# Output-gate projection moved between the samples' score products, last score product and sigmoid moved behind the stage's barrier, prompt stores moved between weight loads

## The chip, the cores and the metric

The kernel runs on one core of a Trainium2 chip. The metric is the time of one execution on the device in microseconds (us); lower is better. The profile names the engines PE (TensorE matmul), PEld (its weight load), DVE (VectorE), ACT (ScalarE), POOL (GpSimd) and SP (SyncE). All data is float32. Each float32 matmul of the program appears in the trace as two records.

## The reference

One layer of a network runs over 512 prompt tokens and over 8 decoding sequences ("samples") of 8 tokens each, 576 tokens in all. Every token row `h` is multiplied by one wide matrix `w_in`, and the parts feed an mLSTM branch, a dilated-window attention branch and two merge gates. What the change touches:

```python
parts = jnp.split(h @ prm['w_in'], split_points, axis=-1)
qk, conv_new = _causal_conv(parts[0], conv_s, prm['conv_w'], prm['conv_b'])   # then silu
ipre = (parts[3] + prm['b_igate'])                                            # 4 heads
logf = jax.nn.log_sigmoid(parts[4] + prm['b_fgate'])                          # 4 heads
hm, C1, n1, m1 = _mlstm_chunkwise(qm, km, vm, ipre, logf, C0, n0, m0)
hm = hm * jax.nn.sigmoid(parts[2])                                            # output gate
...
# per sample and head, for three window groups over cached keys and values
s = jnp.einsum('bthd,btjhd->bthj', q, kg) * (q.shape[-1] ** -0.5)
p, lse = _softmax_lse(jnp.where(valid, s, -inf))
```

Prompt attention over three windows (128, 512 and 2048 with dilations 1, 4, 16), the rolled key and value caches of the samples, and a PEER expert layer complete the step. The prompt's keys and values and the rolled caches are outputs.

## The kernel before

The program is a sequence of blocks. In a block each engine has its own list of instructions, ordered by hand, and semaphores tie them together. A block ends with a barrier over all engines. The token rows are held transposed in `k.hT` (8 slices of 128 features by 576 tokens); token tiles are four of 128 and one of 64 (`NCH` = 5).

**prompt_attention** (355 to 552 us of the trace) runs 16 steps `s`, one for each of 4 token tiles and 4 heads. TensorE does in step `s`: the scores of step `s + 1` (L662), `first_pieces[s]` pieces of projection work, the transposes of the probabilities of step `s` (L676), one more piece, and the product with the values (L683). The transposes wait for VectorE's normalised probabilities (`s_norm`), the value product for ScalarE's copy of the transposes (`s_te`, L720). ScalarE does the exponentials of step `s + 1` (L729) before that copy. Tiles 0 to 3 have 3, 6, 8 and 10 key blocks of 128.

A piece is one unit of **MlstmProjections**: 8 accumulating matmuls into bank 6 or 7, and an eviction by ScalarE (`take`, L600 to L608). The weights come in 8 loads of 1 MB through a ring of two slots (`load`, L571): loads 0 to 3 hold the q/k parts (4 pieces each, L584, 288 columns), loads 4 and 5 the values and 6 and 7 the output gate (5 pieces each, L587, 256 columns). The output gate's pieces are evicted with a sigmoid into `m.o`, all others with a copy. With `first_pieces = [2] * 4 + [1] * 12` steps 0 to 3 take three pieces and steps 4 to 15 two. Load `n` is issued when the last piece of load `n - 2` is done.

On SyncE's queue the stores of the prompt's keys and values (`kT_p` L643, `v_p` L644, three pairs, 1 MB each) follow the eighth load. GpSimd's queue issues three copies of 1 MB each from cache to cache in HBM in every step (`rolls`, L653; the last eight are of 480 KB); these are the rolled caches.

**conv_and_gates** (552 to 657 us) computes three things side by side. VectorE and ScalarE run the causal convolutions, the silu, and the chain of the gate rows. TensorE begins with new-key scores and zeros (L842, L832), then the products of the two gates (L1037: 4 output rows, 512 + 64 columns, one gate after the other), with the score products of **SampleAttention** (`product(n)` for sample `n`, L867) after them. One product is 104 matmuls of 128 columns in three parts whose cached keys arrive in a ring of three slots (1.25, 1 and 1 MB), so part `n` is requested when part `n - 3` has been used. It writes to 32-row groups of the output, four heads side by side. After sample 4 come the transposes of the gate rows (L1049, L1052), then samples 5 to 7. VectorE masks the scores (`masked`, L880 to L884), ScalarE takes their exponentials (L889), and the barrier follows. SyncE also loads the first sample's values (`CG_LOADS`), stores the small output `m_new` and waits until it has landed.

**mlstm_and_merge** (from 657 us) begins with `scores(0)` (L1339 to L1341), the transposes of the samples' probabilities (`sa.turn`, L905, L906, after VectorE's `normalised`), and `sums(0)` (L1356 on). Then the samples' value products, the mLSTM chunks and the merge units alternate. The output block and the expert layer follow to the end.

## Time and profile before

| | us |
|---|---|
| median of 3 runs (lowest, highest) | 2494.43 (2490.22, 2497.33) |
| the profiled execution | 2489.25 |
| its span | 2487.5 |
| PE busy | 2159.1 (87%) |
| DVE busy | 1232.5 (50%) |
| ACT busy | 762.6 (31%) |
| POOL busy | 733.8 (29%) |

The busy shares average over stages with different limits. The expert layer takes the last two thirds of the span, so what matters for the change is read from the two blocks that it touches, between 355 and some 670 us. A row of the trace in time gives start, duration, engine, line, operation, what is written from what, and the count of instructions merged; a bracket gives idle time before it and what ended that.

### The profile page before, as it was taken

The page shows a single profiled execution, that of the slowest core. Times are in us where ns is not written, and L with a number is a line of the kernel's source. Part 1 is how long each engine was busy: PE and PEld are TensorE (multiplying, and loading weights), DVE is VectorE, ACT ScalarE, POOL GpSimd, SP SyncE. Part 2 cuts the span into 40 slices and gives each one's busy share as a digit, 9 for nine tenths or more (in the row PEclk, how much of TensorE's full clock was granted, in tenths as well). Part 3 has the DMA queues.
Part 4 walks back from the last instruction along what each step waited for, and adds up shares of the span by engine and source line. Part 5 has one row for each costly group of instructions (what it writes and reads, how often), then busy time and mean ns, then how long its engine had stood idle before and what let it go on. Part 6 is the DMA issues. An engine that isn't in the chain of part 4 may idle for free.

```text
span 2487.5 us, 25285 instructions
## 1 busy us (share of the span) xinstructions
PE 2159.1 (87%) x9074; PEld 1247.8 (50%) x9074; DVE 1232.5 (50%) x3183; ACT 762.6 (31%) x2197; POOL 733.8 (29%) x694
## 2 busy tenths in 40 slices
PE   6999989997799879999997888787879787978686
PEld 3777448875588545555553443343434333433221
DVE  1000001216233156556666766677676766676764
ACT  2000012242132034444334443343333333333322
POOL 0000001110102014334344444343434352444341
PEclk8999999997699989999999989898989898989899
DMA  9566648888786559999999999999999999999997
GB/s 357 208 242 259 255 168 320 321 299 342 267 298 229 200 225 394 390 396 408 390 381 400 420 403 396 419 416 415 419 413 420 413 412 409 398 420 420 420 419 295
DMA packets 125489, 875.53 MB, mean 352 GB/s; under 512 B 15944, under 2 KB 17256, under 8 KB 40500
## 3 DMA queue, kind: packets, MB, share of 16 engines
q0 software_dynamic: 85760, 691.32, 69.0%
q1 hardware_dynamic: 38652, 182.48, 19.4%
q8 instruction: 71, 1.16, 0.2%
q14 instruction: 54, 0.44, 0.0%
q10 hardware_dynamic: 952, 0.13, 0.0%
HBM read 861.53 MB, written 99.37 MB: 386 GB/s over the span
## 4 chain that ended last, share of the span: by engine, by line
PE 34%; DVE 14%; DMA 13%; issue 2%; ACT 2%; POOL 1%; ACTq 0%; POOLq 0%; DVEq 0%
PE ps L1888 24%; DMA pr_ring<-in_uv,pr_idx 12%; PE ps L1784 3%; DVE pr_ring L2110 3%; PE ps L1824 3%; PE ps L1833 1%; PE ps L1846 1%; PE ps L1806 1%; DVE pr_hot L2090 1%; DVE pr_hot L2094 1%; DVE pr_ind L2071 1%; DVE pr_ind L2068 1%; DVE pr_pick L2097 1%; DVE pr_val L2070 1%; ACT pr_coef L1960 1%
## 5 line engine op out<-in xcount | busy, mean ns | idle before, releaser
L1888 PE MATMUL ps<-pr_ring,pr_diag 128*128 128x512 f32 (+1 forms) x2224 | 1042.8, 623 | 210.5 <-ACT pr_diag L1964 210.3
L1769 POOL DMA_INDIRECT pr_ring<-in_uv,pr_idx x556 | 640.0, 1151 | 956.5 <-PE ps L1888 815.6
L2110 DVE CUSTOM_DVE_ANT_0 pr_ring<-pr_ring,h 128x1024 f32<-128x1024 f32 x556 | 662.7, 1223 | 357.7 <-DMA pr_ring<-in_uv,pr_idx 356.6
L1888 PEld LDWEIGHTS ps<-pr_ring,pr_diag 128*128 128x128 f32 (+1 forms) x2224 | 424.3, 195 | 773.9 <-issue 473.0
L1955 ACT ACTIVATE pr_gel<-pr_dots 128x2 f32<-128x2 f32 x288 | 58.0, 201 | 526.0 <-DVE pr_dots L2110 525.2
L1964 ACT ACTIVATE pr_diag<-ident,pr_coef 128x128 f32<-128x128 f32 x512 | 173.6, 386 | 0.0
L1960 ACT ACTIVATE pr_coef<-pr_gel,pr_wgt 128x1 f32<-128x1 f32 x576 | 138.4, 287 | 27.0 <-ACT pr_gel L1955 0.4
L1784 PE MATMUL ps<-trunk,pr_wq 128*128 128x320 f32 (+2 forms) x544 | 131.7, 396 | 3.0 <-ACT trunk L1990 2.2
L474 PE MATMUL ps<-trunk,ap_ring 128*128 128x288 f32 x384 | 126.3, 411 | 2.9 <-PEq L192 2.9
L475 PE MATMUL ps<-trunk,ap_ring 128*128 128x288 f32 x384 | 125.2, 408 | 0.0
L1784 PEld LDWEIGHTS ps<-trunk,pr_wq 128*128 128x128 f32 x544 | 100.0, 194 | 41.6 <-issue 14.9
L435 POOL DMA_DIRECT2D out_win_s<-in_cache x39 | 19.2, 493 | 328.5 <-PE ps L475 238.1
L474 PEld LDWEIGHTS ps<-trunk,ap_ring 128*128 128x128 f32 x384 | 72.9, 191 | 23.8 <-issue 4.2
L867 PE MATMUL ps<-sa_ring,sa_spread 128*32 128x128 f32 x1664 | 64.5, 316 | 23.4 <-DMA sa_ring<-in_kcacheA 14.4
L475 PEld LDWEIGHTS ps<-trunk,ap_ring 128*128 128x128 f32 x384 | 73.5, 192 | 20.5
L478 PE MATMUL ps<-ap_ring,trunk 128*128 128x512 f32 x192 | 83.6, 594 | 0.0
L697 DVE CUSTOM_DVE_ANT_0 pa_prob<-ps,pa_masks 128x256 f32<-128x256 f32 (+3 forms) x48 | 19.4, 455 | 128.6 <-PE ps L662 128.6
L491 DVE COPY vS<-ps 64x512 f32<-64x512 f32 x3 | 2.1, 693 | 151.9 <-PE ps L466 151.9
L653 POOL DMA_DIRECT2D out_win_s<-in_cache x49 | 23.5, 486 | 175.8 <-PE ps L676 175.6
L1955 ACT ACT_TABLE_LOAD x58 | 74.4, 1283 | 1.1
L587 PE MATMUL ps<-mp_ring,trunk 128*128 128x256 f32 (+1 forms) x320 | 72.6, 380 | 0.0
L379 DVE TENSOR_TENSOR late_rows<-ps,late_bias 128x512 f32<-128x512 f32 x2 | 1.4, 692 | 141.6 <-PE ps L369 141.6
(319 smaller groups left out, 2306.5 us busy)
## 6 DMA issues: line engine op xcount, KB each, us to landing
out_win_s<-in_cache POOLq DMA_DIRECT2D x64, 1020.0 KB, 7.7
sa_ring<-in_cache SPq DMA_DIRECT2D x24, 1024.0 KB, 9.1
side_unit<-in_w_merge SPq DMA_DIRECT2D x32, 768.0 KB, 7.1
late_ring<-in_w_ada SPq DMA_DIRECT2D x8, 2048.0 KB, 17.4
sa_ring<-in_kcacheB SPq DMA_DIRECT2D x16, 1024.0 KB, 7.5
pr_wq<-in_peer_wq SPq DMA_DIRECT2D x16, 1024.0 KB, 8.8
out_win_s<-in_cache POOLq DMA_DIRECT2D x16, 1008.0 KB, 9.5
ap_ring<-in_w_attn_qk SPq DMA_DIRECT2D x6, 2048.0 KB, 21.1
```

The source lines that it names most:

```text
L474: pe.matmul(ps[:, u % 2, 0:TH], wc, rhsT[:, c, 0:TH], **on)
L475: mm = pe.matmul(ps[:, 2 + u % 2, 0:TH], wc, rhsT[:, c, TH:T], **on)
L478: mm = pe.matmul(ps[0:r, u % 2, :], rhsT[:, c, tile_cols(j)], w[:, c, :], **on)
L587: mm = pe.matmul(self.k.ps[0:tile_rows(j), bank, 0:self.WIDE], hT[:, c, tile_cols(j)], w[:, c, :], **on)
L1769: pool.indirect_dma_start(row(n), None, d["uv"], bass.IndirectOffsetOnAxis(ap=idx[:, b % 4, j:j + 1], axis=0)).then_inc(arrived[slot(n)], 16)
L1784: mm = pe.matmul(ps[:, QUERY_BANK, 0:cols.stop - cols.start], e.wq[:, c, piece % 2 * P:(piece % 2 + 1) * P], e.h2T[:, c, cols], start=c == ...
L1824: mm = pe.matmul(ps[:, SIDE_BANK, 0:REST], front.unit[:, u % 2, c, :], k.hT[:, c, rest_cols], start=c == 0, stop=c == KD - 1)
L1888: mm = pe.matmul(ps[0:r, bank + half, :], diag[:, slot(n), 0:r], row(n)[:, o:o + CHUNK], start=h == 0 and j == 0, stop=b == FINAL[i] and j ...
L1955: act.activation(gel[:, o:o + BATCH], dots[:, o:o + BATCH], ACT.Gelu).then_inc(s_gel, 1)
L1960: act.activation(coef[:, o + j:o + j + 1], gel[:, o + j:o + j + 1], ACT.Copy, scale=wgt[:, b % 4, at:at + 1]).then_inc(s_cf, 1)
L1964: act.activation(diag[:, o + j, 0:r], k.ident[:] if i < PT else k.fold[:], ACT.Copy, scale=coef[:, o + j:o + j + 1]).then_inc(s_dg, 1)
L2110: ins = dve.tensor_tensor_reduce(u, u, e.h2[:, BLOCKS[b][0], :], 1.0, 0.0, ALU.mult, ALU.add, dots[:, slot(n):slot(n) + 1])
```

## The change

Five things move.

- MlstmProjections makes 6 loads. The ten output-gate pieces leave the prompt attention; `first_pieces` is `[2] * 4 + [1] * 2 + [0] * 10`, so that steps 4 and 5 keep two pieces and steps 6 to 15 have one, behind the transposes.
- The ten pieces become `output_gate(u)` in conv_and_gates: two before the first sample's product, then one after each of samples 0 to 3, one before each of samples 5 and 6, and two at the end. Their weights have one buffer `ow`, loaded twice. ScalarE evicts them with a copy; one sigmoid over all of `m.o` runs at the head of the next block.
- The score product of sample 7, `masked` and the exponentials move behind the barrier. The first sample's values are loaded there too.
- The two gates' products are written in four 32-row groups of bank 0 (two gates by two halves of 288 tokens), interleaved, where they stood one after the other.
- The three pairs of prompt stores are issued behind weight loads 2, 3 and 4; the store of `m_new` no longer ends the block.

```diff
-        self.loads = 8
+        self.loads = 6
...
-    def load(self, sp):
-        for n in range(self.loads):
+    def load(self, sp, loads):
+        for n in loads:
...
-                out, how = (m.v, ACT.Copy) if n < 6 else (m.o, ACT.Sigmoid)
-                ins = act.activation(out[0:r, j, o:o + self.WIDE], res[0:r, 0:self.WIDE], how)
+                ins = act.activation(m.v[0:r, j, o:o + self.WIDE], res[0:r, 0:self.WIDE], ACT.Copy)
...
-        first_pieces = [2] * 4 + [1] * 12
+        first_pieces = [2] * 4 + [1] * 2 + [0] * 10
         with nc.Block() as block:
             @block.sync
             def _(sp):
-                mp.load(sp)
+                mp.load(sp, range(mp.SLOTS))
                 for g in range(G):
+                    mp.load(sp, range(mp.SLOTS + g, mp.SLOTS + g + 1))
                     sp.dma_start(d["kT_p"][g], a.qk[:, (2 * g + 1) * H:(2 * g + 2) * H, :]).then_inc(s_kv, 16)
                     sp.dma_start(d["v_p"][g], a.v[:, :, g, :]).then_inc(s_kv, 16)
+                mp.load(sp, range(mp.SLOTS + G, mp.loads))
                 sp.wait_ge(s_kv, 16 * 2 * G)
...
+GATES = ((1, 0), (1, 1), (0, 0), (0, 1))
-CG_LOADS = (NS + 1) * SampleAttention.PARTS
+CG_LOADS = NS * SampleAttention.PARTS
...
-                for dst, src in ((state[:], "stateT"), (cw[:], "conv_w"), (wg[:], "w_gates"), (gb[:], "b_gates"),
-                                 (m0[:], "m0"), (carry[:], "c_carry"), (restart[:], "c_restart")):
+                sp.dma_start(wg[:], d["w_gates"]).then_inc(s_wg, 16)
+                for dst, src in ((state[:], "stateT"), (cw[:], "conv_w"), (gb[:], "b_gates")):
                     sp.dma_start(dst, d[src]).then_inc(s_in, 16)
+                sp.dma_start(ow[:], d["w_mlstm"][6]).then_inc(ow_ready, 16)
+                for dst, src in ((m0[:], "m0"), (carry[:], "c_carry"), (restart[:], "c_restart")):
+                    sp.dma_start(dst, d[src]).then_inc(s_in, 16)
+                sa.load(sp, range(sa.SR))
                 for dst, src in ((m.tri[:], "c_tri"), (m.stri[:], "c_stri"), (m.mhg[:], "mh_norm_g")):
                     sp.dma_start(dst, d[src]).then_inc(m.s_const, 16)
-                sa.load(sp, range(sa.SR))
-                sp.dma_start(smask[:].rearrange("p q n -> p (q n)"), d["c_smask"]).then_inc(sa.s_mask, 16)
+                sp.dma_start(sa.smask[:].rearrange("p q n -> p (q n)"), d["c_smask"]).then_inc(sa.s_mask, 16)
                 sa.load(sp, range(sa.SR, 4 * sa.PARTS))
+                sp.wait_ge(s_om, NCH)
+                sp.dma_start(ow[:], d["w_mlstm"][7]).then_inc(ow_ready, 16)
                 sp.wait_ge(s_new, 2)
                 sp.dma_start(d["conv_p"], newp[:]).then_inc(s_out, 16)
                 sp.dma_start(d["conv_s"], news[:]).then_inc(s_out, 16)
-                sa.load(sp, range(4 * sa.PARTS, CG_LOADS))
+                sa.load(sp, range(4 * sa.PARTS, 6 * sa.PARTS))
                 sp.wait_ge(s_mn, 2)
-                sp.dma_start(d["m_new"], mnew[:]).then_inc(s_out, 16)
-                sp.wait_ge(s_out, 48)
+                sp.dma_start(d["m_new"], m.new[:]).then_inc(m.s_new, 16)
+                sa.load(sp, range(6 * sa.PARTS, CG_LOADS))
+                sp.wait_ge(s_out, 32)
...
-                pe.wait_ge(s_in, 7 * 16)
-                for gate in (1, 0):
-                    for part, cols in ((0, slice(0, SEQ)), (1, slice(SEQ, T))):
-                        n = cols.stop - cols.start
-                        for c in range(KD):
-                            mm = pe.matmul(ps[0:H, 2 * gate + part, 0:n], wg[:, c, gate * H:(gate + 1) * H],
-                                           k.hT[:, c, cols], start=c == 0, stop=c == KD - 1)
-                    mm.then_inc(s_gm, 1)
-                    sa.product(pe, 1 - gate)
-                for n in range(2, 5):
+                pe.wait_ge(s_wg, 16)
+                def output_gate(u):
+                    j = u % NCH
+                    if j == 0:
+                        pe.wait_ge(ow_ready, 16 * (u // NCH + 1))
+                    if u >= 3:
+                        pe.wait_ge(s_ot, u - 2)
+                    for c in range(KD):
+                        mm = pe.matmul(ps[0:tile_rows(j), 1 + u % 3, 0:WIDE], k.hT[:, c, tile_cols(j)], ow[:, c, :],
+                                       start=c == 0, stop=c == KD - 1)
+                    mm.then_inc(s_om, 1)
+
+                for step in range(KD):
+                    for j, (gate, half) in enumerate(GATES):
+                        mm = pe.matmul(ps[32 * j:32 * j + H, 0, 0:TH], wg[:, step, gate * H:(gate + 1) * H],
+                                       k.hT[:, step, half * TH:(half + 1) * TH], start=step == 0, stop=step == KD - 1)
+                mm.then_inc(s_gm, 1)
+                output_gate(0)
+                output_gate(1)
+                for n in range(4):
                     sa.product(pe, n)
+                    output_gate(n + 2)
+                sa.product(pe, 4)
                 pe.wait_ge(s_exp, 1)
...
-                for n in range(5, NS):
+                for n in range(5, NS - 1):
+                    output_gate(n + 1)
                     sa.product(pe, n)
+                for u in range(NS, 2 * NCH):
+                    output_gate(u)
...
+                def output_gates(us):
+                    for u in us:
+                        j, o = u % NCH, u // NCH * WIDE
+                        r = tile_rows(j)
+                        act.wait_ge(s_om, u + 1)
+                        act.activation(m.o[0:r, j, o:o + WIDE], ps[0:r, 1 + u % 3, 0:WIDE], ACT.Copy).then_inc(s_ot, 1)
+
+                chain.step(gate_rows(1, fg))
...
-                for b in range(H):
-                    silu(b)
+                output_gates(range(0, 2))
+                silu(0)
+                output_gates(range(2, 3))
+                silu(1)
+                output_gates(range(3, 4))
+                silu(2)
+                silu(3)
+                output_gates(range(4, 5))
                 act.wait_ge(s_rows, 1)
                 for kind in (W_, E_, X_):
                     act.activation(m.rows[:, kind, :], m.rows[:, kind, :], ACT.Exp)
                 act.activation(m.decay[:], m.decay[:], ACT.Exp).then_inc(s_exp, 1)
-                for b in range(H, 2 * H):
-                    silu(b)
-                sa.exponentials(act)
+                output_gates(range(5, 6))
+                silu(4)
+                output_gates(range(6, 7))
+                silu(5)
+                output_gates(range(7, 8))
+                silu(6)
+                silu(7)
+                output_gates(range(8, 2 * NCH))
...
-                sa.masked(dve, chain, smask)
...
                 mg.load(sp, 1)
+                cache(NS)
                 cache(NS + 1)
...
+                sa.product(pe, NS - 1)
                 scores(0)
                 sa.turn(pe)
...
+                act.activation(m.o[:, 0:PT, :], m.o[:, 0:PT, :], ACT.Sigmoid)
+                act.activation(m.o[0:TS, PT, :], m.o[0:TS, PT, :], ACT.Sigmoid).then_inc(m.s_o, 1)
+                sa.exponentials(act)
...
+                sa.masked(dve, chain)
                 sa.normalised(dve, chain)
...
+                    if c == 0:
+                        dve.wait_ge(m.s_o, 1)
```

On TensorE, the last full step of the prompt attention (scores L662/L663, transposes L676/L677, projection pieces L587, values L683/L684). Before:

```order
L662 MATMUL ps<-a_qk 128x256
L662 MATMUL ps<-a_qk 128x512 x2
L587 MATMUL ps<-mp_ring,trunk 128x256 x8
L676 MATMUL ps<-ident,pa_prob 128x128 x10
L587 MATMUL ps<-mp_ring,trunk 128x256 x8
L683 MATMUL ps<-pa_probT,a_v 128x128 x10
```

With the change:

```order
L663 MATMUL ps<-a_qk 128x256
L663 MATMUL ps<-a_qk 128x512 x2
L677 MATMUL ps<-ident,pa_prob 128x128 x10
L587 MATMUL ps<-mp_ring,trunk 128x256 x8
L684 MATMUL ps<-pa_probT,a_v 128x128 x10
```

The piece ahead of the transposes is gone.

On TensorE, the whole of conv_and_gates, from the new-key scores to the next block's first product (L1037/L1058 gates, L867/L870 score products, L1052 with `cg_ow` the output-gate pieces). Before:

```order
L842 MATMUL ps<-qkS 32x64 x24
L832 MATMUL ps<-trunk,sa_spread 32x384 x8
L1037 MATMUL ps<-trunk,cg_wg 4x512 x8
L1037 MATMUL ps<-trunk,cg_wg 4x64 x8
L867 MATMUL ps<-sa_ring,sa_spread 32x128 x52
L1037 MATMUL ps<-trunk,cg_wg 4x512 x8
L1037 MATMUL ps<-trunk,cg_wg 4x64 x8
L867 MATMUL ps<-sa_ring,sa_spread 32x128 x208
L1049 MATMUL ps<-ident,m_rows 128x4 x16
L1049 MATMUL ps<-ident,m_rows 64x4 x4
L1052 MATMUL ps<-m_decay,sel 128x12 x4
L867 MATMUL ps<-sa_ring,sa_spread 32x128 x156
```

With the change (two blocks of rows, the second from the transposes of the gate rows on):

```order
L845 MATMUL ps<-qkS 32x64 x24
L835 MATMUL ps<-trunk,sa_spread 32x384 x8
L1058 MATMUL ps<-trunk,cg_wg 4x288 x32
L1052 MATMUL ps<-cg_ow,trunk 128x256 x16
L870 MATMUL ps<-sa_ring,sa_spread 32x128 x52
L1052 MATMUL ps<-cg_ow,trunk 128x256 x8
L870 MATMUL ps<-sa_ring,sa_spread 32x128 x52
L1052 MATMUL ps<-cg_ow,trunk 128x256 x8
```

```order
L1073 MATMUL ps<-ident,m_rows 128x4 x16
L1073 MATMUL ps<-ident,m_rows 64x4 x4
L1076 MATMUL ps<-m_decay,sel 128x12 x4
L1052 MATMUL ps<-cg_ow,trunk 128x256 x8
L870 MATMUL ps<-sa_ring,sa_spread 32x128 x52
L1052 MATMUL ps<-cg_ow,trunk 128x256 x8
L870 MATMUL ps<-sa_ring,sa_spread 32x128 x52
L1052 MATMUL ps<-cg_ow,trunk 128x256 x8
L1052 MATMUL ps<-cg_ow,trunk 64x256 x8
L1006 UNCONDITIONAL_BRANCH
L1381 UNCONDITIONAL_BRANCH
L870 MATMUL ps<-sa_ring,sa_spread 32x128 x52
```

The output-gate pieces stand between the score products, and the last 52 score matmuls behind the two branches that are the barrier.

On SyncE, the prompt attention's weights and stores. Before:

```order
L571 DMA mp_ring<-in_w_mlstm 128x2048 x8
L643 DMA out_kT_p<-a_qk 128x2048
L644 DMA out_v_p<-a_v 512x1x512
L643 DMA out_kT_p<-a_qk 128x2048
L644 DMA out_v_p<-a_v 512x1x512
```

With the change:

```order
L571 DMA mp_ring<-in_w_mlstm 128x2048 x3
L643 DMA out_kT_p<-a_qk 128x2048
L644 DMA out_v_p<-a_v 512x1x512
L571 DMA mp_ring<-in_w_mlstm 128x2048
L643 DMA out_kT_p<-a_qk 128x2048
L644 DMA out_v_p<-a_v 512x1x512
L571 DMA mp_ring<-in_w_mlstm 128x2048
```

The stores stand between loads that TensorE still needs.

## Rows read from the trace of the kernel before

**Rows 1.** Stretches of the program: busy us per engine, clock, DMA share, GB/s.

```profile
355.00:552.00 197.00, 195.38 (x996) 159.43 (x996) 37.84 (x160) 61.15 (x132) 23.54 (x49) 0.98 0.86 312
552.00:657.00 105.00, 69.93 (x1009) 47.82 (x1009) 45.58 (x142) 20.38 (x30) 9.76 (x7) 0.69 0.79 303
...
900.00:2487.00 1587.00, 1339.93 (x3500) 648.64 (x3500) 1050.91 (x2572) 578.08 (x1797) 659.53 (x574) 0.93 0.99 404
```

**Rows 2.** TensorE in time, one prompt-attention step: start, us, line, operation, count.

```profile
530.91 3.62 PE L587 MATMUL ps<-mp_ring,trunk 128*128 128x256 f32 x16
534.36 1.26 PE L676 MATMUL ps<-ident,pa_prob 128*128 128x128 f32 x10
535.45 3.62 PE L587 MATMUL ps<-mp_ring,trunk 128*128 128x256 f32 x16
538.91 2.39 PE L683 MATMUL ps<-pa_probT,a_v 128*128 128x128 f32 x20
```

**Rows 3.** ScalarE in time, in that same step.

```profile
533.18 1.36 ACT L729 ACTIVATE pa_prob<-pa_prob,pa_nb 128x1280 f32<-128x1280 f32 x1 [2.64 <-DVE pa_nb L702]
...
534.65 1.28 ACT L608 ACT_TABLE_LOAD   x1
...
536.23 1.36 ACT L720 ACTIVATE pa_probT<-ps 128x512 f32<-128x512 f32 x3
```

**Rows 4.** TensorE in time, projection pieces at the start of the prompt attention.

```profile
374.66 7.93 PE L584 MATMUL ps<-trunk,mp_ring 128*128 128x288 f32 x32
...
387.97 7.93 PE L584 MATMUL ps<-trunk,mp_ring 128*128 128x288 f32 x32
...
415.84 4.04 PE L584 MATMUL ps<-trunk,mp_ring 128*128 128x288 f32 x16
...
437.94 3.62 PE L587 MATMUL ps<-mp_ring,trunk 128*128 128x256 f32 x16
```

**Rows 5.** Issue to landing by tile: weights, key stores, value stores.

```profile
DMA to landing us min/median/max: 4.7/9.6/15.8
...
DMA to landing us min/median/max: 20.4/34.7/44.0
...
DMA to landing us min/median/max: 29.8/30.5/42.3
```

**Rows 6.** DMA queues, 510 to 540 us: packets, MB, share of 16 engines.

```profile
q0 software_dynamic: 254, 6.10, 53.6%
q1 hardware_dynamic: 1832, 5.16, 44.0%
```

**Rows 7.** TensorE in time, conv_and_gates to the start of mlstm_and_merge.

```profile
555.58 1.50 PE L842 MATMUL ps<-qkS 128*32 128x64 f32 x48 [3.70 <-PEq L2282]
...
561.08 9.53 PE L1037 MATMUL ps<-trunk,cg_wg 128*4 128x512 f32 x31
...
570.49 3.00 PE L867 MATMUL ps<-sa_ring,sa_spread 128*32 128x128 f32 x101
...
603.04 1.08 PE L867 MATMUL ps<-sa_ring,sa_spread 128*32 128x128 f32 x32 [0.91 <-DMA sa_ring<-in_kcacheB]
...
611.74 1.94 PE L867 MATMUL ps<-sa_ring,sa_spread 128*32 128x128 f32 x32 [0.65 <-DMA sa_ring<-in_kcacheB]
...
656.84 0.45 PE L1339 MATMUL ps<-ident,m_qk 128*128 128x128 f32 x1 [8.72 <-PEq L1000]
```

**Rows 8.** Three engines in time, last score product to first sums.

```profile
648.29 0.56 DVE L880 TENSOR_TENSOR sa_sc<-ps,cg_smask 128x384 f32<-128x384 f32 x1 [18.30 <-PE ps L867]
...
652.91 0.19 ACT L889 ACTIVATION_READ_ACCUMULATOR sa_sc<-sa_sc,sa_nb 128x1 f32 x1
...
657.04 1.36 DVE L896 TENSOR_TENSOR sa_sc<-sa_sc,sa_rden 128x1152 f32<-128x1152 f32 x1
...
663.82 0.69 DVE L1471 TENSOR_TENSOR ml_w<-m_tri,ps 128x512 f32<-128x512 f32 x1 [5.42 <-PE ps L1341]
...
666.59 0.57 PE L1356 MATMUL ps<-m_v,ml_sT 128*128 128x128 f32 x2 [0.32 <-DVE ml_sT L1477]
```

More of the change, by code:

```diff
@@ L1061, in _, with gate_rows @@
                 act.wait_ge(s_gm, 1)
[L1062 to L1063 removed]
+                act.wait_ge(s_in, 6 * 16)
+                def gate_rows(gate, out):
+                    for half in range(2):
+                        o = 32 * GATES.index((gate, half))
+                        ins = act.activation(out[:, half * TH:(half + 1) * TH], ps[o:o + H, 0, 0:TH], ACT.Identity,
+                                             bias=gb[o:o + H, gate:gate + 1])
+                    return ins
+                def output_gates(us):
[5 more added lines that the diff above has]
+                chain.step(gate_rows(1, fg))
                 chain.step(act.activation(e[:], fg[:], ACT.Abs))
```

38 lines of the change are left out of this document (21 added, 17 removed).

## The prediction

> **What bounds the kernel now.** I read the stretches first [rows 1]. In the prompt attention TensorE is busy 195.4 of 197 us at the full clock: every microsecond of matmul taken out shortens the stage, if nothing else is next. In conv_and_gates it is busy 69.9 of 105 us at a granted clock of 0.69, and the DMA share is 0.79: the stage waits for something else. From 900 us on the DMA engines are at 0.99 and 404 GB/s; that part only starts earlier or later, so I carry a shift of the early stages through to the end one to one. Then I read TensorE in time. In a step of the prompt attention one row follows on the other without idle time [rows 2]. In conv_and_gates the score products end in a rhythm, at 604.1 (603.04 + 1.08) and 613.7 us (611.74 + 1.94), each with a bracket that names a key load: 9.6 us for 3.41 MB (1280 + 1024 + 1024 KB), or 357 GB/s [rows 7]. Its end is an idle time of 8.7 us before 656.84 [rows 7], filled with mask, maximum and exponentials (648.3 to 653.1 us) and the barrier [rows 8]. So the change takes work from a stage that TensorE bounds and puts it where the loads of the cached keys do.
>
> **Prompt attention: ten pieces out.** One piece costs 534.36 - 530.91 = 3.45 us of TensorE [rows 2]. Ten are 34.5 us. What is late next is ScalarE. It starts the exponential 2.27 us after the scores end (533.18 against 530.91) and is free again at 534.65, 3.74 us after them [rows 3]. Today a table load of 1.28 us and the eviction follow, then the copy of 1.36 us that the value product needs. The table load is there for the sigmoid; without one it goes, and the copy can end at 3.74 + 1.36 = 5.1 us, with a handover of 0.2 at 5.3 us. TensorE reaches the value product after 1.09 + 3.46 = 4.55 us [rows 2]. It waits 0.7 us in the three steps with ten key blocks that still have a score step ahead, and some 0.5 in the step before them; with six and eight blocks exponential and copy are shorter and I count nothing. Sum: 34.5 - 2.6 = **31.9 us gained**. The normalised probabilities are no limit: the scores of a step end a whole transposition, piece and value product (6.9 us) before the next scores even begin, and take under 5 us.
>
> **The stores between the loads.** Nothing waits for them but the end of the block; queued behind them on SyncE's queue are weight loads 3, 4 and 5. Load 2 is issued at some 379 us, when the first piece of the row at 374.66 ends, and load 3 at 395.7, when the row at 387.97 ends; load 3 is first used at 415.84 [rows 4]. So load 2, the first pair of stores and load 3, 4.2 MB, have 37 us: the queue needs 114 GB/s. Load 4, first used at 437.94 [rows 4], makes it 7.3 MB in 59 us, 124 GB/s. Between 510 and 540 us the same queue moved 5.16 MB of such stores beside 6.10 MB of cache copies [rows 6], 172 GB/s. Against that stand the landing times: loads took 9.6 us (up to 15.8), and stores 20 to 44 us, six behind one another [rows 5]. I take no wait, and up to 17 us for the upper end (below).
>
> By the Trainium skill, page "DMA: Bandwidth & Descriptors", section "Queues, rings and completion order", each DMA engine takes the queues in turn, a packet at a time. The records of 510 to 540 us show 1832 packets on the stores' queue against 254 of the copies [rows 6], so turns between packets as the profile counts them don't describe this trace.
>
> **conv_and_gates.** Counted from its first matmul at 555.58, the zeros end at 5.5 us [rows 7]. The gates cost 9.53 us for the first of two now [rows 7]; interleaved in four 32-row groups they should run side by side, as the score product's do: 101 records of 128 columns in 3.00 us, 30 ns each. 64 records of 288 columns are 64 x 30 x 288/128 = 4.3 us. The bounds are 4.3 and 9.5; I take 4.5, since the score products have the same four-group form, and reach 10 us. Two output-gate units at 3.5 us follow, and the first product at 3.0 ends at 20 us. Its keys queue behind the first `ow` load, 4.4 MB, some 12 us at 357 GB/s from an issue at 2 us, so they are there. From then on a sample needs 3.5 + 3.0 = 6.5 us of TensorE and 9.6 us of loading, so the rhythm of 9.6 us stays and the units hide in it: six samples are 57.4 us. The second `ow` load stands in the same queue, 1.05 MB, 2.9 us. Product 6 ends at 80.3, the last two units at 87.3. The barrier costs 3.7 [rows 7] and a handover 0.2: the next block starts at 91.2, where it started at 101.3 (656.84 - 555.58). **10.1 us gained.** The gate rows' chain on VectorE and ScalarE starts about where it did and is waited for only behind product 4, at 60 us; the silu and GpSimd's scaling of the keys follow the unit at 70 us and end before 87.
>
> **The next block.** Today the first sums start 9.75 us after it (666.59 - 656.84). Then: product 7, 3.0 us, whose keys were requested in product 6 and have 9 us to land; a handover of 0.2; mask to exponentials 4.8 (648.29 to 652.91 + 0.19); normalising 0.2 + 1.4; and from 663.82 to 666.59 2.8 more [rows 8]. That is 12.4 us, **2.7 us lost**. The sigmoid over 2560 elements a row costs 2.8 us at the exponential's 1280 in 1.36 us [rows 3], with two table loads 5.4 us. It hides behind product and mask, 3.0 + 0.2 + 3.1; its cover is 1 us thick. The first sample's values are issued here, behind 3.5 MB of states and merge weights: 7 MB at 357 GB/s are 20 us, about when their product comes.
>
> **DMA.** The prompt attention moves 312 x 197 = 61.5 MB [rows 1], in future 59.4 MB in 165 us, 360 GB/s; a stage under the same mix reached 375 [rows 6], but its first 15 us hold little. The cache copies then end a few microseconds later than TensorE, and the key loads of the next stage start beside them. I take **2 us** for that and for the later values, between 0 and 11.
>
> **Sum.** -31.9 - 10.1 + 2.7 + 2 = -37.3 us, so the profiled execution of 2489.25 becomes 2452. The median of the runs shown, 2494.43, lies 5.2 above that execution, so I forecast a median of **2457 us**.
>
> **The rivals.**
> - *The units are free* (0.12). If the loads run faster while TensorE holds the ring's slots, the stage is TensorE's: 10 + 7 + 7 x 3.0 + 6 x 3.5 + 7 for the gate rows + 7 = 73 us and 4 for the barrier, 14 less than above: 2443. For it: 404 GB/s is possible [rows 1]. Against it: every product's bracket is a load [rows 7].
> - *The queue makes TensorE wait* (0.15). The first three of the old stores' and load's megabytes went at about 100 GB/s, since the median value store took 30.5 us [rows 5]. At 97 GB/s load 3 lands 43 us after 379, 6.6 us late, and load 4 75.7 us after, another 10: 17 us, 2474.
> - *The DMA engines are full* (0.15). At 312/0.86 = 363 GB/s [rows 1] the 59.4 MB need 164 us where some 154 are usable; 10 us of copies run into a stage that loads bound. With the values 3 us late, 11 in place of 2: 2466.
> - *Slower than before* (0.04). Each of loads 3 and 4 waits for the pair ahead of it for the longest landing seen, 44 us, and takes 15.8 itself [rows 5]: load 3 lands at 379 + 60 = 439, 23 us late; the second pair and load 4 take 60 more, 499, where 438 + 23 were wanted, 38 late. 61 - 37 = 24 us slower, 2518. It decides once TensorE's waits for loads pass 37 us in all.
>
> If turns between packets as the page names them held, the 944 packets of load 2, stores and load 3 would need some eight steps' copies, and the result would be this last one or worse; the 7 to 1 of the trace speaks against it.
>
> **How the numbers follow.** The forecast has 0.54. The range takes in the first three rivals and some of their sum: 2440 to 2480; outside stay the slower case and a tail of about 0.08. A difference under 0.3%, 7.5 us, can't be told from none. Faster 0.95, same 0.02, slower 0.03 (the slower rival may stop short of it).
>
> **What would show it.** Right: the prompt attention ends about 32 us earlier with TensorE waits of under 1 us a step for ScalarE's copy; no wait for `mp_ring` loads; products in conv_and_gates still end 9 to 10 us apart, with idle time now 3 us smaller and a granted clock near 1; the gates take under 6 us; the next block starts some 42 us earlier, and its first sums some 39. Wrong: idle time before L584 pieces named after `mp_ring`, a gap longer than 10 us between products, a gate product of 9 us, or `turn` waiting for ScalarE's sigmoid.

## The result and the profile after

| | before | after |
|---|---|---|
| median of the runs shown, us | 2494.43 (2490.22 to 2497.33) | 2478.45 (2467.57 to 2479.41) |
| profiled execution, us | 2489.25 | 2479.41 |
| its span, us | 2487.5 | 2477.6 |

The ratio of the changed kernel to the one before is 0.9938, with a 95% interval of 0.9918 to 0.9959. The forecast was 2457 us, in a range of 2440 to 2480. So the sign and the range held, but the gain is 16 us between the medians (10 us between the profiled executions, and 10 to 20 by the interval) where 37 had been forecast.

Where the gain went can be read by milestones: TensorE's first matmul of a stage, in the profiled executions.

| us | before | after | difference | forecast |
|---|---|---|---|---|
| start to prompt attention | 354.8 | 355.3 | +0.5 | 0 |
| prompt attention | 200.8 | 186.6 | -14.2 | -31.9 |
| conv_and_gates to the first sums | 111.0 | 110.8 | -0.2 | -10.1 + 2.7 = -7.4 |
| first sums to the output projection | 184.6 | 187.8 | +3.2 | |
| output projection to the end | 1636.3 | 1637.2 | +0.9 | +2 (the "DMA" term, which was also meant for the end of the prompt attention) |
| span | 2487.5 | 2477.6 | -9.9 | -37.3 |

Of the 27 us that are missing between the profiled executions, 18 are in the prompt attention and 7 in conv_and_gates. These are the stretches of the changed kernel's trace (busy us per engine, granted clock, DMA share, GB/s), to be held against [rows 1]:

```profile
355.00:541.00 186.00, 164.54 (x836) 132.57 (x836) 37.84 (x160) 47.74 (x115) 23.55 (x49) 0.93 0.90 319
541.00:641.00 100.00, 81.15 (x1089) 63.20 (x1093) 42.27 (x135) 20.57 (x34) 10.44 (x9) 0.88 0.78 305
...
900.00:2477.00 1577.00, 1340.56 (x3489) 647.32 (x3488) 1046.06 (x2565) 575.58 (x1793) 651.96 (x566) 0.93 0.99 404
```

In the prompt attention TensorE has 21 us without work, where it had 1.6. All ten pieces are gone from it (195.4 busy us became 164.5), but the stage is no longer TensorE's. TensorE in time shows where most of that lies (start, us, line, operation, and in brackets the idle time ahead and what ended it); the first row is the last piece that uses load 3, the third is the piece that [rows 4] had at 437.94:

```profile
431.80 4.05 PE L584 MATMUL ps<-trunk,mp_ring 128*128 128x288 f32 x16
...
438.32 0.82 PE L677 MATMUL ps<-ident,pa_prob 128*128 128x128 f32 x6
453.66 6.26 PE L587 MATMUL ps<-mp_ring,trunk 128*128 128x256 f32 x16 [14.53 <-DMA mp_ring<-in_w_mlstm]
```

One wait of 14.53 us for weight load 4, and behind it a piece of 6.26 us where its like take 3.62: 17.2 us together. The times from issue to landing, for the weight loads, the key stores and the value stores (min, median, max), against [rows 5]:

```profile
DMA to landing us min/median/max: 4.8/13.3/39.2
...
DMA to landing us min/median/max: 19.5/26.1/44.0
...
DMA to landing us min/median/max: 21.6/38.8/48.1
```

Load 4 is the 39.2: issued at 414.44, landed at 453.6. Ahead of it in SyncE's queue stand the second key store and the second value store, issued at 396.7 and 398.0; the value store landed at 436.8. Load 4 alone then took 17 us for its megabyte. So of its 39.2 us some 22 are the stores ahead of it and 17 its own. The queues in that stretch, 438 to 454 us (packets, MB, share of 16 engines):

```profile
DMA packets 304, 5.87 MB, mean 367 GB/s; under 512 B 94, under 2 KB 94, under 8 KB 115
...
q0 software_dynamic: 151, 4.90, 85.2%
q1 hardware_dynamic: 153, 0.98, 16.5%
```

The packets stand at one to one, 151 of the copies' queue (q0) and 153 of SyncE's (q1), but the bytes at five to one: the copies' packets are 32 KB on average (about half of them are under 512 B) and the weights' 6.4. The load gets 61 GB/s of 367. The equal counts prove no rule: the same 16 us of the kernel before hold 143 and 144, with a load that took no more than 15.8 us. In the stretch the forecast had used [rows 6], the packets stood at 1 to 7, an average of unlike parts. Cut into six parts of 5 us, it has 504, 514 and 563 packets of the stores' queue to 21, 22 and 44 of the copies' in three of them, and 40, 66 and 145 to 45, 42 and 80 in the others. Where both queues had work, the stores' share was far smaller than the average says.

In conv_and_gates the sequence of TensorE is the one forecast, up to product 4:

```profile
541.85 1.51 PE L845 MATMUL ps<-qkS 128*32 128x64 f32 x48 [4.35 <-PEq L2341]
...
547.34 4.18 PE L1058 MATMUL ps<-trunk,cg_wg 128*4 128x288 f32 x64
551.45 7.17 PE L1052 MATMUL ps<-cg_ow,trunk 128*128 128x256 f32 x32
558.56 3.04 PE L870 MATMUL ps<-sa_ring,sa_spread 128*32 128x128 f32 x104
...
601.80 1.61 PE L870 MATMUL ps<-sa_ring,sa_spread 128*32 128x128 f32 x32 [1.40 <-DMA sa_ring<-in_kcacheB]
603.34 7.92 PE L1073 MATMUL ps<-ident,m_rows 4*128 4x4 f32 x40
611.20 1.88 PE L1076 MATMUL ps<-m_decay,sel 4*128 4x12 f32 x8
613.00 5.11 PE L1052 MATMUL ps<-cg_ow,trunk 128*128 128x256 f32 x16
618.04 3.05 PE L870 MATMUL ps<-sa_ring,sa_spread 128*32 128x128 f32 x104
...
632.13 7.32 PE L1052 MATMUL ps<-cg_ow,trunk 128*128 128x256 f32 x32
640.32 3.04 PE L870 MATMUL ps<-sa_ring,sa_spread 128*32 128x128 f32 x104 [0.87 <-PEq L1006]
```

The gates take 4.18 us (forecast 4.5) where [rows 7] had 9.53 for the first of two, product 0 ends 19.7 us after the stage's start (20) and product 4 at 61.6 (61.2). Then stand 9.7 us of gate-row transposes (L1073, L1076), which my sum had no term for, at a granted clock of half speed, the 1.2 GHz level, and a unit of 5.11 us behind them. While TensorE does that, no slot of the ring comes free and the DMA engines run dry; the second of these stretches holds no more than 0.8 MB:

```profile
603.00:613.00 10.00, 10.00 (x56) 9.60 (x48) 3.89 (x11) 0.00 (x0) 0.00 (x0) 0.50 0.59 224
607.00:620.00 13.00, 13.00 (x120) 11.86 (x124) 0.46 (x2) 0.95 (x2) 0.00 (x0) 0.66 0.14 60
```

Product 5 ends 79.2 us after the start where I had 70.7. An end of the block that costs 0.87 us, where I had 3.7 from [rows 7] (the end of the prompt attention), gives 3 back. From the next block's start to its first sums it is 12.3 us (640.32 to 652.61) for 12.4 forecast from [rows 8]. ScalarE's sigmoid stayed under product and mask: it is over (643.25 + 0.61) before the mask is, and the exponential waits for VectorE.

```profile
640.13 1.28 ACT L1483 ACT_TABLE_LOAD   x1 [0.27 <-PEq L1006]
641.43 1.91 ACT L1483 ACTIVATE m_o<-m_o 128x2048 f32<-128x2048 f32 x1
643.25 0.61 ACT L1484 ACTIVATE m_o<-m_o 64x512 f32<-64x512 f32 x1
643.88 1.28 ACT L892 ACT_TABLE_LOAD   x1
646.70 0.78 ACT L892 ACTIVATE sa_sc<-sa_sc,sa_nb 128x576 f32<-128x576 f32 x1 [1.54 <-DVE sa_nb L887]
```

### The profile page after: what moved, and what is told of

Read it like the earlier page. It is cut to its first block, busy times and chain, and to the rows that moved or that the text cites. A ratio compares the mean times of both kernels' runs of the same rounds, so it can differ in the third digit from the quotient of the medians.

```text
span 2477.6 us, 25280 instructions
## 1 busy us (share of the span) xinstructions
PE 2143.7 (87%) x9074; PEld 1240.3 (50%) x9074; DVE 1232.3 (50%) x3183; ACT 754.7 (30%) x2192; POOL 733.9 (30%) x694
## 4 chain that ended last, share of the span: by engine, by line
PE 36%; DVE 14%; DMA 11%; ACT 2%; issue 2%; POOL 0%; ACTq 0%; POOLq 0%; DVEq 0%
PE ps L1947 25%; DMA pr_ring<-in_uv,pr_idx 11%; PE ps L1843 3%; DVE pr_ring L2169 3%; PE ps L1883 3%; PE ps L1892 1%; PE ps L1905 1%; PE ps L1865 1%; DVE pr_hot L2149 1%; DVE pr_hot L2153 1%; DVE pr_ind L2130 1%; DVE pr_ind L2127 1%; DVE pr_pick L2156 1%; ACT pr_coef L2019 1%; DVE pr_val L2129 1%
## 5 line engine op out<-in xcount | busy, mean ns | idle before, releaser
L1883 PE MATMUL ps<-trunk,side_unit 128*128 128x320 f32 x256 | 71.5, 432 | 0.0
L1254 PE MATMUL ps<-trunk,side_unit 128*128 128x256 f32 x256 | 62.6, 400 | 7.8 <-DMA side_unit<-in_w_merge 7.8
```

What stands on the lines that cost most here:

```text
L1254: mm = pe.matmul(k.ps[:, self.GATE, self.COLS], unit[:, c, :], k.hT[:, c, 0:GROUPED], start=c == 0, stop=c == KD - 1)
L1883: mm = pe.matmul(ps[:, SIDE_BANK, 0:REST], front.unit[:, u % 2, c, :], k.hT[:, c, rest_cols], start=c == 0, stop=c == KD - 1)
```

## The experiments

Each kernel ran beside the kernel before on the same chip: the change on one, e1 to e4 on a second, e5 to e8 on a third, e9 and e10 on a fourth. The kernel before had medians of 2494.43, 2491.40, 2488.46 and 2491.37 us there, so that across these groups the ratios compare better than the medians do. For each I give the stages as in the table above, in us: prompt attention (PA), conv_and_gates to the first sums (CG), first sums to the output projection (ML). The identical first 355 us differ by up to 9 us between profiled executions (348.8 in one, 358.1 in another of the same code up to there), so that stages say more than single spans do; each stage is read from one execution.

| kernel | median, us | ratio to before, 95% | PA | CG | ML |
|---|---|---|---|---|---|
| before | 2494.43 | 1 | 200.8 | 111.0 | 184.6 |
| the change | 2478.45 | 0.9938 (0.9918 to 0.9959) | 186.6 | 110.8 | 187.8 |
| e1: stores last | 2475.11 | 0.9944 (0.9922 to 0.9965) | 186.0 | 111.0 | 185.4 |
| e2: before, stores between | 2504.29 | 1.0054 (1.0033 to 1.0075) | 212.9 | 107.2 | 195.9 |
| e3: no copies in steps 2 to 5 | 2507.42 (one run) | | 209.9 | 110.8 | 191.1 |
| e4: gate rows late | 2477.85 | 0.9939 (0.9917 to 0.9961) | 187.0 | 110.6 | 184.7 |
| e5: stores last, copies early | 2463.14 | 0.9903 (0.9876 to 0.9931) | 166.8 | 107.7 | 187.5 |
| e6: e1 with units back | 2483.49 | 0.9977 (0.9956 to 0.9998) | 201.5 | 96.8 | 190.7 |
| e7: the change, copies early | 2477.78 | 0.9955 (0.9936 to 0.9974) | 177.6 | 112.7 | 185.8 |
| e8: e5, gate rows in three | 2467.69 | 0.9908 (0.9881 to 0.9935) | 166.4 | 102.9 | 193.5 |
| e9: before, copies early | 2494.48 | 1.0012 (0.9992 to 1.0033) | 198.9 | 110.1 | 184.7 |
| e10: e5 with units back | 2487.19 | 0.9979 (0.9959 to 1.0000) | 198.9 | 94.8 | 195.6 |

The first four (e1 to e4) asked what holds the prompt attention and what the stores' new place does.

**e1, stores last.** The change with every store behind the last weight load.

```diff
 mp.load(sp, range(mp.SLOTS))
+mp.load(sp, range(mp.SLOTS, mp.loads))
 ...
-    mp.load(sp, range(mp.SLOTS + g, mp.SLOTS + g + 1))
```

> The changed kernel with one thing put back: all three pairs of prompt stores are issued behind the last weight load (load 5). Queue theory (the stores stand ahead of load 4 on one queue, and that is what TensorE waited for): load 4 lands within 16 us of its issue, the 14.5 us wait ahead of the first value piece and the slow piece behind it (6.3 for 3.6 us) go, the prompt attention ends 17 us earlier than in the changed kernel, and the time is about 2462 us, ratio to the kernel before 0.987. Full-engines theory (the denser cache copies fill the DMA engines, and load 4 would be late behind them without any store): load 4 still lands later than 23 us after its issue, a wait of 8 us or more stays, and the time stays near 2478.

No load was waited for any more, but the stage is as long as before the edit (186.0 us for 186.6), because its end now waits 21.24 us. Load 4 landed 11.1 us after its issue, as the queue theory had it, but the 17 us that it promised did not come. TensorE in time, then SyncE's queue in time (start, us that the issue took), then the view of waits of SyncE (us in total, times, longest):

```profile
511.06 2.50 PE L683 MATMUL ps<-pa_probT,a_v 128*128 128x128 f32 x20
534.80 1.51 PE L844 MATMUL ps<-qkS 128*32 128x64 f32 x48 [21.24 <-PEq L2340]
```

```profile
432.12 46.36 SPq L643 DMA_DIRECT2D out_kT_p<-a_qk  x1
478.52 13.07 SPq L644 DMA_DIRECT2D out_v_p<-a_v  x1
```

```profile
SPq L637 <- DMA out_v_p<-a_v: 42.0, 1, 42.0
```

The DMA engines had no pause in it:

```profile
430.00:480.00 50.00, 49.75 (x283) 40.49 (x282) 16.22 (x63) 16.96 (x37) 8.65 (x18) 1.00 1.02 359
480.00:515.00 35.00, 32.18 (x191) 25.78 (x189) 8.51 (x28) 11.76 (x26) 5.76 (x12) 1.00 0.98 336
515.00:535.00 20.00, 0.20 (x9) 0.23 (x13) 0.00 (x0) 0.00 (x0) 0.24 (x1) 0.55 0.81 324
```

So the load's wait is gone and nothing is won: a second limit of almost the same length stands behind it. The stage moves 59.3 MB, and its closing barrier comes only when they have landed. The issue of the fifth store, too, took 46 us in place of 0.4 to 1.3. In the kernel before, the fifth store behind one another took 17.21 us; that a queue has room for only so much is the likely reason, but nothing here shows it.

**e2, the stores' new place alone, in the kernel before.** It leaves the ten pieces and everything else as they were.

```diff
-    def load(self, sp):
-        for n in range(self.loads):
+    def load(self, sp, loads):
+        for n in loads:
```

> The kernel before with only the stores moved as the change moves them (pair g behind load 2 + g); the ten output-gate pieces stay. Queue theory: load 4 is used at the same time as in the changed kernel (step 6), so the same wait of 13 to 15 us appears, plus 3 us of a slow piece: 2494 + 16 = 2510 us, ratio 1.007. Full-engines theory: up to step 6 the copies are as dense as before, so without the shorter steps no wait: ratio 1.000. If later loads wait as well, over 1.010.

The stores' new place by itself costs 13 us by the ratio (forecast 16), and PA is 12.1 us longer. The wait for load 4 is there, 9.79 us where the theory had 13 to 15:

```profile
451.22 5.60 PE L587 MATMUL ps<-mp_ring,trunk 128*128 128x256 f32 x16 [9.79 <-DMA mp_ring<-in_w_mlstm]
```

The profiled execution is 9 us above this kernel's median. Its ML of 195.9 us has another reason, the clock of the first sums (see e8).

**e3, the change without the copies beside loads 3 and 4.** The copies of steps 2 to 5 are issued in later steps.

```diff
-for _ in range(min(3 if s else 4, len(k.rolls))):
+for _ in range(min((4, 3, 0, 0, 0, 0, 4, 4, 4, 4, 4, 4, 4, 5, 5, 4)[s], len(k.rolls))):
```

> The changed kernel, stores between the loads as it has them, but GpSimd issues no cache copies in steps 2 to 5 and makes up for them from step 6 on (4 or 5 a step for 3). Turns theory (with both queues busy the stores' queue gets a small share of each DMA engine, so it is the copies beside it that make it slow): load 4 lands within 15 us of its issue, no wait at step 6. Rival (stores out of SBUF are slow by themselves, whatever runs beside): load 4 still takes over 25 us, and a wait of 8 us or more stays. The total says little, since copies are moved late.

With the same stores ahead of them the loads landed in 4.8 to 11.7 us, and TensorE waited for none: the stores' bytes alone don't make load 4 late. Nor do the copies alone, since without stores ahead of it (e1) it landed in 11.1 us. With both it took 39.2. The copies thus put off came in at the end and were paid there, with a closing wait of 45.33 us. The weight loads' time to landing, then TensorE in time:

```profile
DMA to landing us min/median/max: 4.8/7.0/11.7
```

```profile
566.69 1.51 PE L845 MATMUL ps<-qkS 128*32 128x64 f32 x48 [45.33 <-PEq L2341]
```

SyncE had nothing left to wait for then, so that the block's end waits for the copies' landing as well, a limit that I had not had in the forecast.

**e4, gate rows late.** This is e1 with the transposes behind the last output-gate unit (the loop over units and products moved ahead of them).

> As e1 (stores last), and in conv_and_gates the transposes of the gate rows (24 matmuls, 9.7 us on TensorE) moved from behind the score product of sample 4 to behind the last output-gate unit. Missed-term theory (my sum left these 9.7 us out: three ring slots hold one sample's keys, so while TensorE does the rows and a unit for 14.6 us the DMA engines go idle for 12): product 5 ends 10 us behind product 4 instead of 17.6, and the stage is 5 to 8 us shorter than in e1: about 2455 to 2457. Rival (the stage is bound by the sum of TensorE's work, so the place of the rows doesn't matter): within 1.5 us of e1.

Behind product 4 the DMA engines no longer pause, and product 5 ends 12 us after it where it was 17.6. From the stage's start to product 7 it is 95.6 us, where the change had 98.5. But product 7 itself then ran at a granted clock of 0.51:

```profile
634.10 4.28 PE L1077 MATMUL ps<-ident,m_rows 4*128 4x4 f32 x40
638.32 1.06 PE L1080 MATMUL ps<-m_decay,sel 4*128 4x12 f32 x8
640.70 5.77 PE L869 MATMUL ps<-sa_ring,sa_spread 128*32 128x128 f32 x104 [1.33 <-PEq L1005]
```

5.77 us in place of 3.04 give the 3 us back. The missed-term theory had 5 to 8 us less than e1; the ratio is 0.9939 for e1's 0.9944. Moving the transposes is no gain by itself.

The next six asked whether both limits together can be taken away, and what the ten pieces are worth.

**e5, stores last and 13 copies early.** The copies move into the projections ahead of the prompt attention:

```diff
-    dst, src = k.rolls.pop()
-    pool.dma_start(dst, src).then_inc(k.s_roll, 16)
+    for _ in range(2 if u % 3 == 0 else 1):
+        dst, src = k.rolls.pop()
+        pool.dma_start(dst, src).then_inc(k.s_roll, 16)
```

> This is the kernel with all stores behind the last weight load (e1_stores_last, 2475.1 us), and with 13 more of the DRAM-to-DRAM cache copies issued before pair attention, in the attention's projection stage (two in place of one at every third unit). In e1 pair attention's weight loads were on time, and its end waited 21.2 us for the transfers to land. Theory A, that pair attention is set by the bytes which must have landed at its closing barrier: 13 copies of 0.52 MB are 6.8 MB; at the 340 GB/s of that stretch they are 20 us of it. The closing wait falls from 21.2 to under 3 us, the output stage starts 17 to 20 us earlier measured from pair attention's start, no wait of TensorE for a load; the projection stage has its DMAs mostly idle and loses at most 2 us. Time 2454 to 2460 us. Theory B, that the closing wait is that of the stores' own late issue (they stand last in their queue): the wait stays at 15 us or more, time 2470 to 2476. Theory C, that copies move the collision into the projection stage: its weight loads come late there, pair attention starts 5 us or more later, time 2465 to 2475.

Theory A held, with a time 3 us above its range: no wait of the prompt attention for a load, a closing wait of 1.40 us, and a PA of 166.8 us, 34.0 under the kernel before (whose closing wait was 3.70).

```profile
525.79 2.50 PE L684 MATMUL ps<-pa_probT,a_v 128*128 128x128 f32 x20
529.69 0.88 PE L845 MATMUL ps<-qkS 128*32 128x64 f32 x48 [1.40 <-PEq L2341]
```

My size for a copy was wrong by half: the copies' queue carried 46.56 MB in e1's stage and 32.98 here, so 13 copies are 13.6 MB, 1020 KB each, and not 6.8. Nor are the DMA engines mostly idle in the projections, as I had it: their share there is 0.55 to 0.70 in the kernel before. Part of the gain is paid ahead: TensorE's stretch of the modulation matmuls that runs through the projections is 229.5 us long (76.3 to 305.8) where it was 224.2, with waits of 1.90 and 2.92 us for weights of that stage. That is theory C, at its lower end of 5 us. The kernel has the lowest median of all. PA, CG and ML together take 462.0 us for the change's 485.2; less the 5 us paid ahead that is 18 us. The medians differ by 15 us and the ratios to before, which set the change's other chip aside, by 0.0035 or 9 us, with intervals that overlap; against e7 on the same chip it is 14.6 us (2463.14 to 2477.78).

**e7, copies early, stores still between.** The change with e5's edit alone.

> This is the change itself with only the 13 copies moved ahead of pair attention; the stores stay between the weight loads. The copies issued in steps 0 to 6 of pair attention keep their density (they are taken from the end of the list). Theory A, turns between the queues delay load 4 whatever the total: TensorE waits for load 4 as before, 10 to 16 us, and the stage's end is not waited for; cg starts 0 to 4 us earlier than with the change. Time 2473 to 2478 us. Theory B, that the total of bytes delays load 4: the wait falls below 5 us, time 2458 to 2465.

The time is the change's; but load 4's wait fell from 14.53 to 8.76 us, between my two theories:

```profile
455.90 5.76 PE L588 MATMUL ps<-mp_ring,trunk 128*128 128x256 f32 x16 [8.76 <-DMA mp_ring<-in_w_mlstm]
```

Load 4 landed in 33.4 us and load 5 in 40.3. The delay doesn't go with the stage's total, since 13.6 MB less did not take it away. Why it became 6 us smaller stays open. PA is 9.0 us shorter than with the change, and its end is not waited for (1.40 us); 5.8 us are paid ahead, in the projections (75.6 to 305.6 us, 230.0 for 224.2). With e1 this gives the order of things: stores last alone gains nothing that can be told, copies early alone gains nothing (0.9955 for the change's 0.9938), and the two together bring 9 to 15 us.

**e6 and e10, the ten pieces back.** e6 is e1, e10 is e5, each with ten pieces and two loads returned to the prompt attention, and no output-gate units in conv_and_gates. Grouped gates, product 7 behind the barrier and the late sigmoid stay.

```diff
-self.loads = 6
+self.loads = 8
 ...
-first_pieces = [2] * 4 + [1] * 2 + [0] * 10
+first_pieces = [2] * 4 + [1] * 12
```

> This is e1_stores_last (2475.1 us) with the ten output-gate pieces back in pair attention's TensorE stream, with their two weight loads (2 MB more through the loads' queue) and no weights loaded or output-gate units computed in the output stage. The grouped gates, the last score product and the mask behind the barrier and the late sigmoid stay. Theory A, that pair attention in e1 is set by the bytes to land, so that TensorE's pieces there are free: the stage lengthens by the 2 MB alone, 6 us, with the closing wait falling from 21.2 to below 5 us; the output stage without units between its products shortens by 15 to 22 us (the units behind the last product and the transposes' slow rows). Time 2460 to 2466 us, faster than the change itself. Theory B, the forecast's, that the ten pieces cost pair attention 34 us and cost the output stage 10 less than they did: time 2485 to 2500 us.

> This is e5_copies_early (2463.1 us) with the ten output-gate pieces and their two loads back in pair attention, as e6_units_back (2483.5) is to e1_stores_last (2475.1). In e5 pair attention took 166.8 us, set by TensorE. Theory A, the pieces' full price shows where the bytes are out of the way: pair attention is 200 to 202 us, the output stage is 87 to 88 us in place of 98.4, and the time is 2478 to 2486 us, so that the move of the pieces is worth 15 to 23 us here and was worth 8 beside all copies. Theory B, that e5's gain over e1 is the copies' own and the pieces matter no more: 2466 to 2472 us.

In e10 theory A held, with a time 1 us above its range. PA is 198.9 and CG 94.8; in e5 they are 166.8 and 107.7. So moving the pieces takes 32.1 us from the one and adds 12.9 to the other, and with what follows it is worth 0.0076 of the time, 19 us, between the ratios, or 24 between the medians (2487.19 to 2463.14). Beside the late bytes, e6 against e1, it is worth 15.5 in PA and costs 14.2 in CG, and the ratios differ by 0.0033, 8 us. In both pairs ML is longer with the pieces back, by 8.1 and 5.3 us, which is the clock of the first sums (see e8) and part of these 19 and 8. Both of e6's theories missed: by A the pieces were free in PA, by B they cost 34, and they cost half of that, as far as the bytes left room. The forecast's price for the pieces on TensorE was right; what hid it was a limit next to it.

e6 shows the other half too. Without units CG is 14 us shorter than before the change, so grouped gates and the moved product are worth those 14, and in the change the units spend them. Its whole time is only 0.0023 (6 us) below before, since its ML is 6.1 us longer than before. I had expected CG to hide the units between products; it does so in part only.

**e8, gate rows in three parts.** e5 with tiles 0 and 1 behind product 3, 2 and 3 behind product 4, 4 with the decay behind product 5.

> This is e5_copies_early with the gate-row transposes of the output stage in three parts, tiles 0 and 1 behind product 3, tiles 2 and 3 behind product 4, tile 4 with the decay behind product 5, in place of all behind product 4. In the change the transposes stood in one piece of 9.8 us at a granted clock of 0.5 to 0.8, and the DMA engines had nothing to do from about 608 to 620 us. Theory A: with each part behind a product's weight wait the DMA keeps working and the parts lie in the wait: product 4's end to product 5's end falls from 17.6 us to 11 to 12 us, and the whole is 5 to 8 us below e5. Theory B: TensorE is what sets this stretch (units, products and transposes together); the transposes cost their 5.3 us at full clock wherever they stand, and the gain is 0 to 3 us.

CG fell by 4.8 us to 102.9, nearly as theory A had it, but the whole is not below e5 (2467.69 for 2463.14, with intervals that overlap): ML rose by 6.0, since the first sums and the next matmuls ran at the 1.2 GHz level. The stretch behind the first sums, first in e5 and then in e8:

```profile
637.40:645.00 7.60, 7.60 (x101) 7.17 (x104) 2.16 (x14) 3.22 (x8) 0.00 (x0) 0.95 0.96 359
```

```profile
634.20:642.00 7.80, 7.80 (x39) 7.77 (x37) 0.65 (x6) 1.55 (x3) 0.00 (x0) 0.50 0.95 356
642.00:652.00 10.00, 10.00 (x141) 8.32 (x144) 5.02 (x25) 2.43 (x5) 0.00 (x0) 0.50 0.03 10
```

The profiled executions of e2, e6 and e10 show the same loss, a granted clock of 0.50 in the first 15 us of sums and an ML of 195.9, 190.7 and 195.6 us; the other kernels ran these sums at 0.88 to 1.00. What the clock costs there is shown; what brings it about is open. TensorE's pauses ahead of the sums (9.5 of 12.2 us busy in e8, 10.0 of 12.4 in e5) look like the reason, but don't tell the kernels apart: the kernel before was busy for 9.44 of the last 12.5 us and ran its sums at 0.98 and more, e2 for 9.45 and ran them at 0.50. Nor need e8's loss be in each of its executions: two took 2462.4 and 2462.8 us, four 2467.5 to 2469.5, and the profiled one is the longest.

**e9, copies early in the kernel before.** The control for e5: is the gain the copies' own?

> This is the kernel before with only the 13 cache copies moved ahead of pair attention, as in e5_copies_early (2463.1 us, 25 us under its before). Theory A: pair attention of before is set by TensorE (200.8 us, closing wait 3.7 us), so bytes taken out of it give at most the 2 us of the closing wait; with them the copies' share of e5's gain is nearly nothing without the change: 2486 to 2494 us at a before of 2490, ratio 0.997 to 1.001, pair attention 198 to 201 us. Theory B: the copies slow TensorE's stage in before too, through late loads or the last stores, and moving them is worth by itself what it gave e5 over e1 (12 us): ratio 0.994 to 0.996, pair attention 188 to 192 us.

It is not: the ratio is 1.0012, and PA is 198.9 us, shorter by 1.9 and no more, as the closing wait fell from 3.70 to 1.40. Taking bytes out of a stage that TensorE sets gives nothing; it pays only together with the pieces.

## Why the prediction was partly wrong

The step that failed is the one that priced the prompt attention as TensorE's once the pieces are out. The stores between the loads were given no wait, and the bytes that must land were given 2 us in all. The runs showed 17.2 us for the first (the change) and 19 us for the second (e1). The two overlap, so that taking away one leaves the other. The third error is a term left out in conv_and_gates, of 7 us.

- **What bounds the kernel** was read rightly for the kernel before (e9: fewer bytes shorten PA by 1.9 us only) and not far enough for the changed one. "Every microsecond of matmul taken out shortens the stage, if nothing else is next" was the right sentence; two other limits were next, 17 and 19 us behind the point where TensorE alone would have ended.
- **Ten pieces out, -31.9 us:** right in size. The stage without other limits became 34.0 us shorter (e5, 2.3 of them in the closing wait) and 32.1 (e5 against e10). The table loads went, and ScalarE's copy was waited for 0.26 to 0.31 us a time, four times, where I had 0.5 to 0.7.
- **Stores between the loads, "I take no wait":** the first half of the step that failed. It cost 14.53 us and a slow piece, 17.2 in all. The rate of [rows 6] came from a stretch in half of which the copies' queue had little to do. The landing times of [rows 5] spoke against it, and the rival built on them was right to a microsecond on load 4: at 97 GB/s it lands 75.7 us after 379, that is at 454.7, and it landed at 453.6. It named 17 us in all, 2474, the nearest of the cases to the result, and had 0.15. That is in part luck. It had one rate for the whole queue and so load 3 late by 6.6 us, which landed 2.3 us in time (the first 4.2 MB went faster than its 97 GB/s, the next slower), and without the load's wait the time was the same (e1).

  By the Trainium skill, page "DMA: Bandwidth & Descriptors", section "Queues, rings and completion order", an engine takes the queues in turn, a whole packet at a time, and a packet is typically some 9 to 17 descriptors. Whether the profile counts such groups, no run here shows. So neither the 1 to 7 on which I dismissed the rule nor the one to one at 438 to 454 us decides on it. My estimate by the rule, "some eight steps' copies", took the profile's packets for the page's, and its own division is off: at 96 packets a step, 944 are ten steps.
- **DMA, 2 us between 0 and 11; "the DMA engines are full", 2466:** the second half of that step. The mechanism was real, and its size too small. Even without the load's wait the bytes end the stage at 186 us (e1), where TensorE alone needs 167: 19 us and not 10. The rival had counted the engines' rate, and not that the closing barrier waits until copies and stores have landed (e1, e3).
- **conv_and_gates, -10.1:** it was -2.8 to the next block (98.5 for 101.3). Gates, first product, rhythm and barrier were right or better; missing was a term for the gate-row transposes. I had counted 7 us for them in the rival "the units are free" and left them out of the forecast's own sum, taking their TensorE time for hidden in the loads. It isn't, because the ring was full and nothing was being loaded.
- **The next block, +2.7:** 12.3 us for 12.4. The sigmoid stayed hidden.
- **After the sums:** +3.2 and +0.9 for the +2.

The two stages, 18 and 7 us, make 25 of the 27. That 2478 lies in the range is owed to the rivals that widened it, and not to the sum.

## What to carry to other kernels

When work leaves the engine that bounds a stage, compute the stage's length by the next two resources before the gain is written down, the DMA bytes that must have landed at its closing barrier among them; two limits that lie close hide one another, so that each repair alone shows next to nothing in the time (e1, e7) and both together show (e5). A queue's rate must be read from a stretch in which its neighbour is busy too: here the average was 172 GB/s, and the load got 61 beside copies of larger packets. That the size of the packets sets the share is likely, but no experiment varied it. A place that is "hidden behind loads" hid here only while the ring had a free slot; look for the DMA share falling to nothing.

## What the runs showed of the hardware

- A 1 MB weight load took 4.7 us at its shortest (before, e1). The same load 4 took 11.1 us without stores ahead of it (e1), at most 11.7 without copies beside it (e3), and 39.2 with both; at the head of its queue it then moved at 61 GB/s of 367.
- Issuing a store took SyncE 46.36 us behind four others (e1) and 17.21 in the kernel before, against 0.4 to 1.3 in the change.
- The end of conv_and_gates took TensorE 0.87 us. The end of the prompt attention, where semaphores are cleared too, took 1.40 us in the kernels whose last copies had been issued some 40 us earlier or more (e5, e7, e8, e9, e10), 3.7 to 4.8 with copies in the last steps, and it waits for transfers in flight (21.24 us in e1, 45.33 in e3).
- The same matmuls ran at either level of the clock: product 7 in 3.04 us and at 0.51 in 5.77 (e4), the first sums at 0.88 to 1.00 and in e2, e6, e8 and e10 at 0.50, with an ML 5 to 11 us longer than in the kernel beside it.
